# One 256-column matmul without a use in iterations 40 to 65 of the first attention

## What is computed

```python
for l in range(DEPTH):                      # 2 layers
    proj = rms_norm(x, attn_norm[l]) @ w_in[l]
    h_mla, h_diff, h_ch = jnp.split(proj, [IN_MLA, IN_MLA + IN_DIFF], axis=-1)
    o_mla = rms_norm(mla_attention(h_mla, ...), mla_out_norm[l])      # 6 heads, latent
    o_diff = diff_attention(h_diff, ...)                              # 6 heads, two maps each
    o_ch = rms_norm(chunk_attention(h_ch, ...), chunk_out_norm[l])    # 4 heads, chunked
    x = x + jnp.concatenate([o_mla, o_diff, o_ch], axis=-1) @ w_out[l]
    x = x + conv_ffn(rms_norm(x, ffn_norm[l]), ...)
# in each attention, for a block of 128 queries and the keys up to it:
    s = scores + mask or bias
    p = jax.nn.softmax(s, axis=-1)
    o = p @ v
```

## Time and profile before

| | |
|---|---|
| median of three runs | 3150.83 us |
| the three runs | 3150.83, 3158.27, 3150.15 us |
| the profiled execution | 3151.19 us |
| its span, first to last instruction | 3149.5 us |
| mean granted TensorE clock | 0.984 |
| TensorE matmul busy | 3071.1 us, 98% of the span |
| VectorE, ScalarE, GpSimd busy | 41%, 25%, 43% |

### The profile page before, as it was taken

One profiled execution on the slowest core, in us unless ns is written; L12 is line 12 of the kernel. 1 busy time (PEld: TensorE's weight loads), 2 busy tenths in 40 slices (PEclk: granted clock), 3 DMA queues, 4 the chain that ended last, 5 costly groups with the idle time before them and its releaser, 6 DMA issues.

```text
span 3149.5 us, 40217 instructions
## 1 busy us (share of the span) xinstructions
PE 3071.1 (98%) x13996; PEld 2412.1 (77%) x13996; DVE 1276.8 (41%) x2913; ACT 801.5 (25%) x1799; POOL 1363.8 (43%) x924
## 2 busy tenths in 40 slices
PE   7999999999999999999999999999999999999998
PEld 6777788887777888887666868888676667688885
DVE  4484535344674433445614531111536226311123
ACT  2354212122362211213333131100223332300012
POOL 4222555554214555553223645555342235455552
PEclk9898999999999999999999999999999999999999
DMA  7322566665315666663233646666442236565662
GB/s 246 94 91 84 181 193 193 194 199 162 94 58 159 186 201 193 192 203 108 91 97 114 215 147 199 197 194 193 139 148 92 90 108 196 157 195 190 186 203 92
DMA packets 136517, 494.06 MB, mean 157 GB/s; under 512 B 15280, under 2 KB 15536, under 8 KB 136112
## 3 DMA queue, kind: packets, MB, share of 16 engines
q0 software_dynamic: 66240, 241.20, 25.0%
q1 hardware_dynamic: 68544, 245.40, 24.1%
q10 hardware_dynamic: 1584, 5.40, 0.5%
HBM read 489.84 MB, written 2.10 MB: 156 GB/s over the span
## 4 chain that ended last, share of the span: by engine, by line
PE 94%; DVE 2%; ACT 1%; issue 1%; DMA 1%; POOL 0%; ACTq 0%; POOLq 0%; DVEq 0%
PE ps L514 26%; PE ps L515 24%; PE ps L516 24%; PE ps L745 3%; PE ps L770 3%; PE ps L692 3%; PE ps L715 2%; PE ps L641 1%; PE ps L643 1%; PE ps L642 1%; PE ps L705 1%; PE ps L758 1%; PE ps L911 1%; PE ps L939 0%; PE ps L780 0%
## 5 line engine op out<-in xcount | busy, mean ns | idle before, releaser
L514 PE MATMUL ps<-hi,w_hi 128*128 128x512 f32 x3216 | 1287.5, 400 | 13.9 <-DVE lo L1043 7.5
L515 PE MATMUL ps<-hi,w_lo 128*128 128x512 f32 x3216 | 1261.2, 392 | 0.0
L516 PE MATMUL ps<-lo,w_hi 128*128 128x512 f32 x3216 | 1260.3, 392 | 0.0
L487 POOL TENSOR_TENSOR w_lo<-w_raw,w_hi 128x1024 fp32r<-128x1024 f32 x460 | 1106.7, 2406 | 97.2 <-DMA w_hi<-weights 87.6
L482 POOL DMA_DIRECT2D w_hi<-weights x460 | 261.1, 568 | 1643.6 <-PE ps L516 1519.8
L514 PEld LDWEIGHTS ps<-hi,w_hi 128*128 128x128 f32 x3216 | 608.2, 189 | 219.2 <-issue 77.3
L516 PEld LDWEIGHTS ps<-lo,w_hi 128*128 128x128 f32 x3216 | 608.5, 189 | 130.1
L515 PEld LDWEIGHTS ps<-hi,w_lo 128*128 128x128 f32 x3216 | 609.0, 189 | 118.9 <-issue 0.2
L1133 DVE CUSTOM_DVE_ANT_0 pr<-ps,kc 128x128 f32<-128x128 f32 (+2 forms) x160 | 65.3, 408 | 323.0 <-PE ps L745 323.0
L1820 ACT ACTIVATE ps<-hb,col 128x512 f32<-128x512 f32 x88 | 68.6, 782 | 381.2 <-DVE hb L1072 381.2
L1555 DVE SCALAR_TENSOR_TENSOR x<-x,ps 128x512 f32<-128x512 f32 x64 | 43.9, 688 | 287.1 <-PE ps L516 287.1
(11 more groups left out here) (316 smaller groups left out, 3133.6 us busy)
## 6 DMA issues: line engine op xcount, KB each, us to landing
w_raw<-weights SPq DMA_DIRECT2D x460, 512.0 KB, 3.5
w_hi<-weights POOLq DMA_DIRECT2D x460, 512.0 KB, 3.8
x<-xt SPq DMA_DIRECT2D x8, 256.0 KB, 10.3
out<-x SPq DMA_DIRECT2D x8, 256.0 KB, 2.0
kc<-k ACTq DMA_DIRECT2D x1, 1281.0 KB, 5.6
bias<-relb ACTq DMA_DIRECT2D x2, 512.0 KB, 5.1
bias<-relb ACTq DMA_DIRECT2D x1, 1024.0 KB, 5.1
praw<-pt ACTq DMA_DIRECT2D x2, 512.0 KB, 3.5
```

The costliest lines, as they stand in the source:

```text
L487: nc.gpsimd.tensor_tensor(wlo[s][:, :], raw[s][:, :], whi[s][:, :].bitcast(F32), ALU.subtract).then_inc(w_split, 1)
L514: nc.tensor.matmul(out_ap, w[0], xx[0], start=first, stop=False)
L515: nc.tensor.matmul(out_ap, w[1], xx[0], start=False, stop=False)
L516: return nc.tensor.matmul(out_ap, w[0], xx[1], start=False, stop=last)
```

## The change

In iterations 40 to 65 the filling work, empty so far, is one float32 matmul of 256 columns: the identity as the stationary operand, the mask as the moving one, into bank 2 of PSUM, where nobody reads it. Before the first of them, TensorE waits once until bank 2 is free. Each layer gets 26 of them. The three last score products are those of iterations 60 to 62, so that in iterations 63 to 65 the added matmul stands at the head of the iteration.

```diff
                     elif it in ITEM_AT:
                         item(ITEM_AT[it])
+                    elif 40 <= it < 66:
+                        if it == 40:
+                            pe.wait_ge(d_free[2], q.freed(2))
+                        nc.tensor.matmul(ps[:, 2, 0:256], ident, kc1[:, 0:256], start=True, stop=True)
```

## The result

The changed kernel takes 3171.52 us in the median of five runs (3167.36 to 3173.52), the kernel before 3150.74 us (3150.15 to 3158.27). The ratio is 1.0062, with a 95% interval of 1.005 to 1.0075: slower by 20.8 us by the medians (19.5 by the ratio), where 17.5 were forecast, and inside the range. The profiled execution of the changed kernel took 3173.52 us, the one of before 3151.19.

A forecast was written before the change was run, and what follows sets the result against it. TensorE was taken to set the pace: 3151.19 us profiled + 19.1 for the added matmuls - 1.6 from the clock = 3168.7, less 0.36 to the runs' median, gives 3168.3 us. Range: 3162 to 3174 us.

The forecast's parts named there:

- The price of one matmul: Each added 256-column matmul on TensorE costs 0.455 us, the middle of 0.42 and 0.49.
- The bare loads: Rival: the identity's two loads show at each added matmul, 0.14 us each, 11.8 us more: 3180 us; chance 0.06.
- The prediction's own argument against bare loads: Score products grow evenly by 0.21 us per 128 columns, claimed to leave no room for bare loads.
- How many are on the path: Of 26 per layer, the 21 in iterations 40 to 60 are paid, 19.1 us in all; iterations 61 to 65 are hidden.
- just hidden: Iterations 61 and 62: two matmuls, 0.91 us, fit TensorE's 0.98 us wait for task 59's copy during ScalarE's table loads.
- TensorE sets the pace: In iterations 40 to 60 TensorE itself paces the loop, 5.49 us from one 512-column score to the next.
- the rival of hidden waits: VectorE and ScalarE pace iterations 40 to 60, hiding the matmuls: 3145.6 us, chance 0.04; half hidden some 3158, chance 0.06.
- What the clock gives back: At the loop's end and the dense product, a shifted clock fall gives a net -1.6 us over both layers.
- The first half of this step: The clock holds 2.4 GHz to the last added matmul, iteration 65, saving 1.7 us in each layer's last tasks.
- The second half: The clock falls over the chunk transposes, costing 1.8 us per layer at the dense product, in layer 0 as before.
- the clock stays up throughout: Rival: no clock fall from loop's end into the dense product, worth 5.2 us: 13.9 us cost, 3164.7 us; chance 0.12.
- the clock falls where it falls now: Rival: the clock falls ahead of the last sums, task 63's transpose about 1.0 us late per layer: 3171.9 us; chance 0.15.

The follow-up runs named there:

- the repeated execution: The changed kernel, unaltered, run and profiled once more against the kernel before: 3171.97 us against 3150.11, ratio 1.0062.
- the kernel with only the waits filled: Kernel before plus the added matmul in iterations 61 to 65, once ahead of the first chunk transposes, three times ahead of fifth and sixth: 3146.19 us, ratio 0.9978.
- both fillings: The changed kernel plus the matmul once ahead of the first chunk transposes, three times ahead of fifth and sixth: 3165.01 us, ratio 1.0045 to the kernel before.

## Why the prediction was right

**The price of one matmul.** 0.455 us was taken, between 0.42 and 0.49; 0.433 was measured in the latent heads and 0.48 net in the chunked ones. Of the 21, 15 stand behind a score of a latent head and 6 behind one of a chunked head: 15 x 0.433 + 6 x 0.48 = 9.38 us, which is the lag that the table has for each layer. The bare loads, priced as a rival, are real where the score has 64 rows: 0.20 us ahead of the added matmul. Most of it is not new, since the transposes behind it are relieved of 0.15. In the 15 latent iterations there are none: 512 columns cost 0.857 us and 256 cost 0.433, which leaves 0.01 us beside the columns. The prediction's own argument against bare loads was weaker than it says, since even steps of 0.21 us say nothing of a cost that each score product has once; what the score's rows did leave for it is 0.28 - 0.21 = 0.07 us. The Trainium skill's rule (TensorE: Matmul & The Clock Gate, Part 3, The mechanism), that a load overlaps only a matmul of another row group, doesn't hold here: with all rows of the array used before and after, there is no bare load, and it is where the rows in use change that 0.20 us shows. The same section also has loads into a background weight buffer pulled ahead, and the full-height rows would fit that.

**How many are on the path.** Right: 2 x 9.38 us by the lag table, against 19.1 predicted. The 21 alone cost 18.6, and the last five alone nothing. The two in iterations 61 and 62 were said to be "just hidden", 0.91 against 0.98 us; task 59's sum now follows at once on the transpose, and starts 0.08 us after the end of ScalarE's copy (0.06 in the kernel before), so the room was used up to within 0.1 us, and that "just hidden" came out is in part luck.

**TensorE sets the pace.** Right, and the rival of hidden waits is out: the period grew by 1.73 us, and by 3.43 with twice the columns.

**What the clock gives back.** The first half of this step held: the clock stayed up to the last sums and beyond, and the tail gained 1.57 and 1.59 us (1.7 predicted). The second half was right in kind and unsure in size. The fall was expected over the chunk transposes, and with it 1.8 us of cost in each layer, in layer 0 the same as before. It came in the wait ahead of the sixth chunk's transposes, at about 283.2 us, and lasted over twelve dense matmuls in the first execution and over some five in the repeated one. From the first chunk transpose on, layer 0 lost 1.03 us more than the kernel before and layer 1 2.74 (0 and 1.8 were set); in the repeated execution layer 0 gained 0.53 and layer 1 lost 1.22. So the clock cost 0.6 us in one execution and gave 2.5 in the other, where 1.6 were forecast: how long it stays low behind the fall isn't settled by the program, and the prediction gave one number for it. What it would be worth undisturbed, 5.2 us, was well sized: the traces show 4.9 us in the kernel with only the waits filled, and 13.8 us of cost for both fillings, where the rival "the clock stays up throughout" had 13.9.

**The sum.** 18.8 us for the matmuls stand in both executions; with the clock the two attentions cost 19.4 us in the one and 16.3 in the other, against 17.5 forecast. The medians (20.8 and 21.9 us) lie above both, and what is more comes from elsewhere in the program, for which the range had allowed 1 to 2 us; that the total came within 3.2 us of the forecast is luck in part. By the total alone, 3171.5 us, one would have chosen the rival "the clock falls where it falls now", which had 3171.9. The trace rules it out: the granted clock is 1.00 over the last sums in both layers. Of the chances, the cases above 3160.3 us have 0.57 + 0.12 + 0.15 + 0.06 = 0.90, and not 0.94.

## What to carry to other kernels

An added matmul on an engine that sets the pace costs its time: at 256 and 512 columns 0.21 us for each 128, with its loads hidden if the matmul before it uses the same rows of the array. In a wait it costs nothing up to the wait's length. So fill only the waits: here 12 such matmuls in each layer ahead of results that other engines still owed kept the clock up and gained 0.22% (0.12 to 0.32), while 21 in the full part of the loop lost 0.6%. Fill up to the start of the dense work: filling that stopped short moved the fall of the clock to the start of that work, where half of the low time was lost, and no gain could be shown.

One profiled execution gives the price of what the program fixes, here to 0.01 us, and not of what the clock does: for that, take a second one.

## What the runs showed of the hardware

- A float32 matmul of 256 columns with all 128 rows used before and after it adds 0.43 us, one of 512 columns 0.86 and one of 32 columns 0.175 us: at 32 columns the columns alone no longer set the price.
- After a matmul that uses 64 of the rows, one that uses all 128 takes 0.20 us more at either width (0.63 to 0.43, and 0.34 to 0.14).
- In the changed kernel the clock stayed at 2.4 GHz over 12 us in which TensorE was busy for 8.8, and fell in the wait of 1.42 us behind them, at the same place in both layers and in the repeated execution.
- With the last five iterations unfilled (the kernel before and the kernels with iterations 40 to 60 alone and with 21 in a row) the clock fell ahead of the last sums in all six profiled stretches and was low for 10.2 or 17.1 us. With them filled by 256 columns it fell only behind them, in five of six, for 3.4 or 6.8 us. With the waits up to the dense product filled too, 16.9 of 18 us busy, it fell in none of four.
- In the runs beside the experiments the kernel before spread from 3146 to 3163 us, while its first five runs lay from 3150 to 3158, and its median from 3150.1 to 3152.5: a median of a few runs is good to some 2 us here. The spread goes with the clock: the runs below 3149 us have a mean granted clock of 0.984 to 0.987, those above 3157 us 0.980 or 0.981.
